# A hybrid decoder block in float32 on one core: 21 of 24 output pairs of the ma, mb and sb projections by seven block products

## The chip, the cores and the metric

The kernel runs on one core of one Trainium2 chip. The metric is device time in microseconds (us) of one execution, the median of several. Engines are named as the profile names them: PE is the tensor engine (PEld its weight loads), DVE the vector engine, ACT the scalar engine, POOL the general engine, SP the sync engine, which issues most DMAs.

## What is computed

A sequence of 512 tokens with 2048 channels, with 16 learned tokens in front (528 in all), goes through one layer. All is float32.

```
hn = rms_norm(h, norm_g)                       # h: 16 meta tokens, then x
z  = hn @ w_in                                 # 2048 x 14336
xa, sa, vb, gb, sb, ma, mb = split(z)          # seven times 2048 columns
ya = rg_lru(causal_conv4(xa)) * silu(sa)       # branch A, gates by 128 x 128 heads
pa = ya @ w_proj_a
yb = causal_conv31(vb * sigmoid(gb))           # branch B
yb = silu(layer_norm(yb)) * silu(sb)
pb = yb @ w_proj_b
h  = h + (sigmoid(ma) * pa + sigmoid(mb) * pb) @ w_out
out = rms_norm(h, final_g)[16:]
```

## The kernel before

Channels lie on the 128 partitions, in 16 tiles; tokens lie along the free dimension. A float32 product is made of three passes of type float32r: every operand is cut into a high and a low part, and hi x hi, lo x hi and hi x lo are summed in PSUM. The normalised input stays in SBUF as x_hi and x_lo, 16 tiles of 528 columns; ya, later yb, as y_hi and y_lo, 16 tiles of 512.

Weights stream in chunks of 512 KB (4 input tiles x 256 output columns). SP loads a chunk into one of RING = 2 slots of raw once the low part of the chunk two before is cut; ACT cuts w_hi from it (cut_hi, L537) once the matmuls of the chunk two before are done; DVE cuts w_lo (cut_lo, L784); PE runs multiply (L369): for 4 input tiles and 2 output tiles first the two passes with w_hi (16 matmuls), then, after a wait for w_lo, the pass with w_lo (8 matmuls). Two output tiles are a pair; four chunks make a pair. Counting semaphores (hi_ready, lo_ready, multiplied) hold chunk numbers, so each engine runs its own queue in code order.

The stages, in the order of the code:

- *Eight branch bodies* of 16 chunks: xa, sa, gb, vb for one pair each. xa, gb and vb are computed for all 528 tokens, as two halves of 264 columns (all_tokens), sa for 512 (x_tokens). Beside them DVE runs the two causal convolutions (conv_b_taps for the pair before, 31 taps, spread by the table TAPS), the recurrence (a scan), and the cut of ya (cut, L796 and L799). Before each of the chunks 8 to 11 PE runs a gate_round (L398), for which c_hi and c_lo must be cut from the short convolution. At the end gate_vb (L981) waits for the whole body's matmuls. The results of the long convolution are spilled to DRAM by POOL.
- *Four a_body:* for each pair the ma projection (x_tokens) and the product of ya with w_proj_a (y_tokens); the sigmoid of ma times pa is spilled. The first also finishes the long convolution of the last pair. The mean of the layer norm comes from a matmul with a constant matrix (L440), the variance later (L478), followed by Sqrt on ACT (L698) and a reciprocal on DVE (L1027) in the first b_body.
- *Four b_body:* sb and mb (x_tokens), the layer norm, the two silu and the cut of yb into y_hi and y_lo.
- *Two bodies of w_proj_b* (y_tokens) with merge, which cuts the merged sum into the x tiles.
- *The output product:* tokens become the stationary operand (x_hi, x_lo), w_out the moving one (L508); the last quarter of w_out is kept as y_hi, y_lo and used at the end (L522), followed by the residual and the last norm.

## Time and profile before

| | us |
|---|---|
| median of 3 runs | 1856.15 |
| lowest, highest | 1855.87, 1856.15 |
| span of the profiled execution | 1854.9 |
| PE busy | 1835.9 |
| PE weight loads busy | 1606.7 |
| DVE busy | 1085.7 |
| ACT busy | 556.3 |
| moved by DMA | 201.55 MB |

The profile is of one execution. Its busy times add durations, and a matmul's duration includes the time until its result has left the array, so successive matmuls overlap; the distance between their starts tells what one costs. The chain of waits is followed back from the last instruction. In the timeline a number of instructions of one form that follow each other is one row, and the idle time before it and what ended it stand in brackets.

### The profile page before, as it was taken

How to read it: one execution, taken by the hardware profiler on the slowest of the kernel's cores; microseconds unless marked ns; L12 is line 12 of the kernel's file. 1: busy time of each engine (PE TensorE's matmuls, PEld its weight loads, DVE VectorE, ACT ScalarE, POOL GpSimd, SP SyncE). 2: the span in 40 equal slices, each digit the busy share in tenths (PEclk: the TensorE clock that was granted, in tenths of full speed). 3: DMA queues.
4: the chain of work that ended last, by engine and by line, in shares of the span. 5: the costliest groups of instructions: out<-in, count | busy, mean ns of one | idle time of the engine just before them, and what ended most of it. 6: DMA issues, size and time to landing. Idle time of an engine off the chain costs nothing.

```text
span 1854.9 us, 26126 instructions
## 1 busy us (share of the span) xinstructions
PE 1835.9 (99%) x10220; PEld 1606.7 (87%) x10220; DVE 1085.7 (59%) x1446; ACT 556.3 (30%) x716; POOL 82.7 (4%) x82
## 2 busy tenths in 40 slices
PE   8999999999999999999999999999999999999998
PEld 7899999999999999988888888888888888888886
DVE  7978787879797979786224243434334433433441
ACT  6542333232423242422213223222222221212322
POOL 5500000000000000000000000000000000000000
PEclk9999999999999999999999999999999999999999
DMA  5233323233323323233633333233332333336422
GB/s 187 80 97 92 99 89 107 90 97 96 101 91 94 104 85 102 90 102 115 210 106 114 102 112 103 91 102 91 95 98 90 101 125 124 114 114 210 145 88 91
DMA packets 169445, 201.55 MB, mean 109 GB/s; under 512 B 6192, under 2 KB 153776, under 8 KB 168752
## 3 DMA queue, kind: packets, MB, share of 16 engines
q1 hardware_dynamic: 163360, 176.68, 30.0%
q0 software_dynamic: 6032, 24.12, 3.9%
q8 instruction: 38, 0.62, 0.1%
q14 instruction: 15, 0.12, 0.0%
HBM read 188.19 MB, written 12.58 MB: 108 GB/s over the span
## 4 chain that ended last, share of the span: by engine, by line
PE 95%; DVE 3%; ACT 1%; issue 0%; DMA 0%; SPq 0%; DVEq 0%; ACTq 0%
PE psum L369 84%; PE psum L508 7%; PE psum L522 2%; PE psum L398 1%; DVE x_lo L874 1%; DVE w_lo L784 1%; DVE region L1103 0%; DMA raw<-in_w_in 0%; DVE region L843 0%; ACT w_hi L537 0%; DVE total L882 0%; DVE region L839 0%; ACT wide L568 0%; DVE x_lo L1097 0%; ACT region L773 0%
## 5 line engine op out<-in xcount | busy, mean ns | idle before, releaser
L369 PE MATMUL psum<-x_hi,w_hi 128*128 128x264 f32 (+1 forms) x2560 | 717.1, 329 | 5.0 <-issue 2.8
L369 PE MATMUL psum<-x_lo,w_hi 128*128 128x264 f32 (+1 forms) x2560 | 715.8, 328 | 0.0
L784 DVE TENSOR_TENSOR w_lo<-raw,w_hi 128x1024 fp32r<-128x1024 f32 x288 | 357.0, 1241 | 559.2 <-ACT w_hi L537 557.1
L537 ACT ACTIVATE w_hi<-raw 128x1024 fp32r<-128x1024 f32 x288 | 305.3, 1060 | 1110.0 <-PE psum L369 1030.6
L369 PEld LDWEIGHTS psum<-x_hi,w_hi 128*128 128x128 f32 x2560 | 432.0, 189 | 50.5 <-issue 4.0
L369 PEld LDWEIGHTS psum<-x_lo,w_hi 128*128 128x128 f32 x2560 | 431.6, 188 | 43.9 <-issue 0.5
L369 PE MATMUL psum<-x_hi,w_lo 128*128 128x264 f32 (+1 forms) x2560 | 458.4, 327 | 2.8 <-DVE w_lo L784 2.8
L369 PEld LDWEIGHTS psum<-x_hi,w_lo 128*128 128x128 f32 x2560 | 386.4, 188 | 47.0 <-DVE w_lo L784 3.4
L818 DVE SCALAR_TENSOR_TENSOR region<-region,conv_cols 128x512 f32<-128x512 f32 x480 | 326.6, 745 | 0.0
L369 PE MATMUL psum<-y_hi,w_hi 128*128 128x512 f32 x512 | 199.8, 390 | 0.0
L369 PE MATMUL psum<-y_lo,w_hi 128*128 128x512 f32 x512 | 199.3, 389 | 0.0
L369 PE MATMUL psum<-y_hi,w_lo 128*128 128x512 f32 x512 | 126.4, 389 | 0.0
L369 PEld LDWEIGHTS psum<-y_hi,w_hi 128*128 128x128 f32 x512 | 96.1, 188 | 20.4 <-issue 0.2
L369 PEld LDWEIGHTS psum<-y_lo,w_hi 128*128 128x128 f32 x512 | 96.1, 188 | 20.3 <-issue 0.2
L369 PEld LDWEIGHTS psum<-y_hi,w_lo 128*128 128x128 f32 x512 | 96.1, 188 | 19.9
L508 PE MATMUL psum<-w_hi,x_hi 128*128 128x512 f32 x192 | 75.6, 394 | 0.0
L508 PE MATMUL psum<-w_hi,x_lo 128*128 128x512 f32 x192 | 75.3, 392 | 0.0
L1196 DVE TENSOR_TENSOR w_lo<-raw,w_hi 128x1024 fp32r<-128x1024 f32 x24 | 29.4, 1224 | 75.4 <-ACT w_hi L759 75.3
L759 ACT ACTIVATE w_hi<-raw 128x1024 fp32r<-128x1024 f32 x24 | 25.4, 1060 | 91.4 <-PE psum L508 51.6
L508 PE MATMUL psum<-w_lo,x_hi 128*128 128x512 f32 x192 | 48.3, 393 | 0.0
L508 PEld LDWEIGHTS psum<-w_hi,x_hi 128*128 128x128 f32 x192 | 36.1, 188 | 8.5
L508 PEld LDWEIGHTS psum<-w_lo,x_hi 128*128 128x128 f32 x192 | 36.1, 188 | 8.2
(150 smaller groups left out, 1000.7 us busy)
## 6 DMA issues: line engine op xcount, KB each, us to landing
raw<-in_w_in SPq DMA_DIRECT2D x224, 512.0 KB, 3.5
raw<-in_w_proj_a SPq DMA_DIRECT2D x32, 512.0 KB, 3.4
raw<-in_w_proj_b SPq DMA_DIRECT2D x32, 512.0 KB, 3.4
raw<-in_w_out SPq DMA_DIRECT2D x32, 512.0 KB, 3.8
region<-in_x_channels SPq DMA_DIRECT2D x8, 512.0 KB, 7.5
conv_b_spill<-region POOLq DMA_DIRECT2D x8, 512.0 KB, 3.2
gated_a_spill<-wide POOLq DMA_DIRECT2D x8, 512.0 KB, 3.5
region<-conv_b_spill POOLq DMA_DIRECT2D x4, 1024.0 KB, 10.8
```

The source lines that it names most:

```text
L369: last = pe.matmul(psum[:, bank, 0:width], weights[:, p % RING, k, m * P:(m + 1) * P], operand[part][:, 4 * group + k, t0:t0 + width], sta ...
L398: last = pe.matmul(psum[:, 6 + g, 0:HALF], weights[:, g, n // 2, :], part[:, :], start=weights is gate_hi and part is c_hi, stop=weights i ...
L508: last = pe.matmul(psum[:, banks + t, :], part[:, 2 * g + k, META + t * P:META + (t + 1) * P], weights[:, k, :], start=g == 0 and k == 0 a ...
L522: last = pe.matmul(psum[:, 4 * (LAST % 2) + t, :], part[:, j, META + t * P:META + (t + 1) * P], weights[:, j, :], start=j == 0 and part is ...
L537: act.activation(w_hi[:, p % RING, :], raw[:, p % RING, :], ACT.Copy).then_inc(hi_ready, 1)
L759: act.activation(to, raw[:, i % RING, :].rearrange("p (k n) -> p k n", k=2), ACT.Copy)\
L784: dve.tensor_tensor(w_lo[:, p % RING, :], raw[:, p % RING, :], w_hi[:, p % RING, :].bitcast(F32), ALU.subtract).then_inc(lo_ready, 1)
L818: ins = dve.scalar_tensor_tensor(conv_b[:, t, :], moved, w, conv_b[:, t, :], ALU.mult, ALU.add)
L874: dve.scalar_tensor_tensor(x_lo[:, j, META:T], channels[:, j, :], params[:, j, NORM_G:NORM_G + 1], x_hi[:, j, META:T].bitcast(F32), ALU.mu ...
L1196: dve.tensor_tensor(lo, raw[:, i % RING, :].rearrange("p (k n) -> p k n", k=2), hi.bitcast(F32), ALU.subtract).then_inc(lo_ready, 1)
```

## The change

Seven block products take the place of the eight of a 2 x 2 block multiplication. A pair's 2048 x 256 weights are cut into four blocks, by input half (8 tiles each) and output tile; the 512 tokens are cut into two halves of 256. The first STD = 3 pairs of the order ma, mb, sb are made as before; the other NV = 21 are units of seven products (A11, S2, S1, S3, A12, A22, S4), each over 8 input tiles with 256 columns. S1 to S4 are sums of weight blocks and are made on DVE for each unit. The token-side sums t_hi, t_lo (four blocks) are made once: t_sums, t_hi_of and t_lo_of in the branch bodies 1 to 7 and in the first plain chunks. They lie where y_hi and y_lo lie; so ya is spilled uncut by POOL and loaded and cut later (load_ya, ya_cut_hi, ya_cut_lo).

Three PSUM banks serve a unit. S2, S3 and A22 accumulate in one bank, A11 and A12 in another, S1 and S4 in the third, and between the products the intermediate values are read: copy_e1 and gate_c11 on ACT, read_u2, read_c22 (u3, then C22), read_c21 and read_c12 on DVE. PE waits for e1, u2, u3 and C22 in between. Weight blocks are loaded with 1 MB each into region, which the branch stage had used for its work tiles; the product operands have four slots, two of them in the unused quarter of the x tiles (cut_slots).

ma, mb and sb times yb are spilled. The layer norm reads the spilled convolution pair by pair into ln, once for the variance (centre_for_variance, square_ln, add_squares in units 1 to 9) and once for yb (centre, scale, silu_ln, gate_yb, from unit 14 on). Silu takes the place of a sigmoid and a product. Then follow 32 chunks of w_proj_a with ya, during which yb is loaded and cut into the x tiles, and 32 chunks of w_proj_b (x_tokens) with the merge, which now cuts into the y tiles. The output product takes y_hi, y_lo as the stationary operand and keeps its last quarter in the x tiles. The long convolution of the last pair runs beside 12 chunks with its own table of taps.

The core of the diff:

```diff
-        y_hi, y_lo = sb("y_hi", [P, CT, SEQ], F32R), sb("y_lo", [P, CT, SEQ], F32R)
+        t_hi, t_lo = sb("t_hi", [P, 4, KH, HS], F32R), sb("t_lo", [P, 4, KH, HS], F32R)
+        y_hi, y_lo = (t[:, :, :, :].rearrange("p b j n -> p (b j n)").rearrange("p (k s) -> p k s", k=CT)
+                      for t in (t_hi, t_lo))
...
+        def cut_slots(s):
+
+
+            if s < RING:
+                return [w[:, s, :].rearrange("p (r h n) -> p r h n", r=4, h=2) for w in (w_hi, w_lo)]
+            r = 4 * (s - RING)
+            return [x_part[:, r:r + 4, META + HS:].rearrange("p r (h n) -> p r h n", h=2) for x_part in (x_hi, x_lo)]
...
-        B_A, B_N, B_B, B_O = PAIRS, PAIRS + QUADS, PAIRS + 2 * QUADS, PAIRS + 2 * QUADS + CT // 8
-
+        STD, NV = 3, 3 * PAIRS - 3
+        C0 = PAIRS * BODY
+        W0 = C0 + 4 * STD
+        A0 = W0 + 7 * NV
...
+        def chunk_free(n):
+
+
+            if W0 <= n < W0 + 4:
+                return min(n, W0)
+            if A0 <= n < A0 + RING:
...
+            def load_blocks(v, h):
+
+
+                if v < 2:
+                    if v == 0:
+                        sp.wait_ge(ya_ready, CT)
+                    else:
+                        sp.wait_ge(vb_gated, CT)
+                        sp.wait_ge(conv_b_spilled, 16 * PAIRS)
+                        sp.wait_ge(summed, CT)
+                        sp.wait_ge(t_lo_ready, 2 * KH)
+                elif h == 0:
+                    sp.wait_ge(s4_ready, v - 1)
+                else:
+                    sp.wait_ge(lo_ready, W0 + 7 * (v - 1))
+                b = 2 * (v % 2) + h
+                sp.dma_start(blocks[:, b], w_in_v[:, KH * h:KH * (h + 1), ds(w_column(STD + v), 256)])\
+                    .then_inc(block_loaded[b], 16)
...
+            def product(v, q, bank, operand, more):
+
+
+                n = W0 + 7 * v + q
+                hi, lo = cut_slots(slot(n))
+
+                def passes(weights, parts, first, last):
+                    for k in range(KH):
+                        for part in parts:
+                            ins = pe.matmul(psum[:, bank, 0:HS], weights[:, k // 2, k % 2, :], operand(part, k),
+                                            start=first and k == 0 and part == 0, stop=last and k == KH - 1,
+                                            skip_group_check=more)
+                    return ins
+
+                pe.wait_ge(hi_ready, n + 1)
+                passes(hi, (0, 1), not more, False)
+                pe.wait_ge(lo_ready, n + 1)
+                passes(lo, (0,), False, True).then_inc(multiplied, 1)
...
+            def unit(v):
+
+
+                w = STD + v
+                a, b, c = (3 * (w % 2) + n for n in range(3))
+                if v < 2:
+                    pe.wait_ge(o_gated, v + 2)
+                    pe.wait_ge(vb_gated, CT)
+                else:
+                    pe.wait_ge(c11_ready, v - 1)
+                product(v, A11, a, x_block(0, 0), False)
+                wait(pe, c21_ready, v - 1)
+                if v == 0:
+                    pe.wait_ge(t_hi_ready, 2 * KH)
+                    pe.wait_ge(t_lo_ready, 2 * KH)
+                product(v, S2, b, t_block(T_T2), False)
+                wait(pe, c12_ready, v - 1)
+                product(v, S1, c, t_block(T_N1), False)
+                if v == 0:
+                    pe.wait_ge(summed, CT)
+                    pe.wait_ge(average_ready, 1)
+                    pe.matmul(psum[:, 7, :], average[:, :], total[:, :], start=True, stop=True).then_inc(mean_ready, 1)
+                pe.wait_ge(u2_ready, v + 1)
+                product(v, S3, b, t_block(T_T3), True)
+                if v == PAIRS + 1:
+                    pe.wait_ge(summed, 2 * CT)
+                    pe.matmul(psum[:, 6, :], average[:, :], total[:, :], start=True, stop=True).then_inc(var_ready, 1)
+                pe.wait_ge(e1_ready, v + 1)
+                product(v, A12, a, x_block(1, 0), True)
+                pe.wait_ge(u3_ready, v + 1)
+                product(v, A22, b, t_block(T_T4), True)
+                pe.wait_ge(c22_ready, v + 1)
+                product(v, S4, c, x_block(1, 1), True)
...
+            for w in range(STD):
+                if w == 1:
+                    pe.wait_ge(vb_gated, CT)
+                elif w == 2:
+                    pe.wait_ge(o_gated, 1)
+                for g in range(4):
+                    multiply(0, C0 + 4 * w + g, x_tokens((3 * (w % 2), 3 * (w % 2) + 1)), g)
+            for v in range(NV):
+                unit(v)
...
+            def operand_hi(v, q):
+
...
+                else:
+                    act.wait_ge({S1: s1_ready, S2: s2_ready, S3: s3_ready, S4: s4_ready}[q], v + 1)
+                act.wait_ge(multiplied, chunk_free(n))
...
+            def unit(v):
+                for q in range(7):
+                    if q == 1:
+                        if v:
+                            gate_c11(v - 1)
+                        else:
+                            gate_std(STD - 1)
+                    if q == 4:
+                        copy_e1(v)
+                        if v:
+                            gate_rest(v - 1)
+                    if q == 5 and STD + v > 2 * PAIRS:
+                        silu_ln(STD + v - 2 * PAIRS - 1)
+                    operand_hi(v, q)
+                    if q == 4 and v == PAIRS + 1:
                         act.wait_ge(var_ready, 1)
                         act.activation(psum[:, 6, :], psum[:, 6, :], ACT.Sqrt, bias=eps).then_inc(std_ready, 1)
-                    if p in (1, 9) and not (first and p == 1):
...
+            def t_sums(j):
+
...
+                r1 = steps(dve.tensor_tensor(sums_a, x_tile(x_hi, j), x_tile(x_lo, j), ALU.add))
+                r2 = steps(dve.tensor_tensor(sums_b, x_tile(x_hi, plus(j, KH)), x_tile(x_lo, plus(j, KH)), ALU.add))
+                steps.done(r1)
+                n1 = steps(dve.tensor_tensor(half(sums_a, 0), half(sums_a, 0), half(sums_a, 1), ALU.subtract))
+                steps.done(r2)
+                dve.tensor_tensor(half(sums_a, 1), half(sums_a, 1), half(sums_b, 1), ALU.subtract)\
+                    .then_inc(t_summed, 1)
+                steps.done(n1)
+                t2 = steps(dve.tensor_tensor(half(sums_b, 1), half(sums_b, 1), half(sums_a, 0), ALU.add))
+                steps.done(t2)
+                dve.tensor_tensor(half(sums_b, 0), half(sums_b, 0), half(sums_b, 1), ALU.subtract)\
+                    .then_inc(t_summed, 1)
...
+            def sum_s2(v):
+
+
+                a11, a21, a12, a22, s3 = winograd_operands(v)
+                dve.wait_ge(s1_ready, v + 1)
+                dve.tensor_tensor(a11, a11, a21, ALU.add).then_inc(s2_ready, 1)
...
+            def read_c22(v):
+
+                w = STD + v
+                dve.wait_ge(multiplied, W0 + 7 * v + S3 + 1)
+                dve.tensor_tensor(u3, bank(v, 1), e1, ALU.subtract).then_inc(u3_ready, 1)
+                dve.wait_ge(u3_ready, v + 1)
+                dve.wait_ge(o_spilled[w % 2], 16 * (w // 2))
+                dve.tensor_tensor(quarter(v, 1, 1), u3, bank(v, 2), ALU.subtract).then_inc(c22_ready, 1)
+
...
+            def unit(v):
+                i = STD + v - 2 * PAIRS - 1
+                if v:
+                    read_c22(v - 1)
+                operand_lo(v, A11)
+                sum_s2(v)
+                if 2 <= v <= PAIRS + 1:
+                    add_squares(v - 2)
+                operand_lo(v, S2)
+                if v:
+                    read_c21(v - 1)
+                if i >= 0:
+                    centre(i)
+                operand_lo(v, S1)
+                if v:
+                    read_c12(v - 1)
+                if i >= 0:
+                    scale(i)
+                operand_lo(v, S3)
+                if 1 <= v <= PAIRS:
+                    centre_for_variance(v - 1)
+                operand_lo(v, A12)
+                sum_s4(v)
+                read_u2(v)
+                operand_lo(v, A22)
+                if v == 0:
+                    dve.wait_ge(mean_ready, 1)
+                    dve.memset(total[:, :], 0.0).then_inc(total_cleared, 1)
+                    dve.wait_ge(total_cleared, 1)
+                if v == PAIRS + 1:
+                    dve.wait_ge(std_ready, 1)
+                    dve.reciprocal(psum[:, 6, :], psum[:, 6, :]).then_inc(rstd_ready, 1)
+                    dve.wait_ge(rstd_ready, 1)
+                if v + 1 < NV:
+                    sum_s3(v + 1)
+                if i >= 0:
+                    gate_yb(i)
+                operand_lo(v, S4)
+                if v + 1 < NV:
+                    sum_s1(v + 1)
```

## Rows read from the trace of the kernel before

**Rows 1.** The page: busy time by engine, and the span in 40 slices.
```profile
PE 1835.9 (99%) x10220; PEld 1606.7 (87%) x10220; DVE 1085.7 (59%) x1446; ACT 556.3 (30%) x716; POOL 82.7 (4%) x82
PEclk9999999999999999999999999999999999999999
GB/s 187 80 97 92 99 89 107 90 97 96 101 91 94 104 85 102 90 102 115 210 106 114 102 112 103 91 102 91 95 98 90 101 125 124 114 114 210 145 88 91
```

**Rows 2.** The chain that ended last: start us, us, what.
```profile
82.61 7.47 PE psum L369 x48
...
643.16 0.72 PE psum L398 x6
...
650.46 5.86 PE psum L369 x48
...
898.30 0.86 PE psum L440 x2
...
1141.42 527.83 PE psum L369 x2304
1669.25 133.03 PE psum L508 x576
1802.28 44.49 PE psum L522 x192
```

**Rows 3.** Timeline of PE and ACT: start us, us, instruction; chunk starts.
```profile
788.18 0.40 PE L369 MATMUL psum<-x_hi,w_hi 128*128 128x512 f32 x1
793.73 0.39 PE L369 MATMUL psum<-x_hi,w_hi 128*128 128x512 f32 x1
...
1003.21 0.39 PE L369 MATMUL psum<-y_hi,w_hi 128*128 128x512 f32 x1
1003.41 1.06 ACT L537 ACTIVATE w_hi<-raw 128x1024 fp32r<-128x1024 f32 x1 [3.89 <-PE psum L369]
1008.65 0.40 PE L369 MATMUL psum<-x_hi,w_hi 128*128 128x512 f32 x1
```

**Rows 4.** Timeline of DVE: start us, us, instruction, idle before.
```profile
639.91 0.43 DVE L858 TENSOR_TENSOR c_lo<-region,c_hi 128x264 fp32r<-128x264 f32 x1
640.25 2.73 DVE L818 SCALAR_TENSOR_TENSOR region<-region,conv_cols 128x512 f32<-128x512 f32 x4
...
788.38 1.32 DVE L981 TENSOR_TENSOR region<-region,psum 128x528 f32<-128x528 f32 x2 [4.04 <-PE psum L369]
...
797.00 4.06 DVE L818 SCALAR_TENSOR_TENSOR region<-region,conv_cols 128x512 f32<-128x512 f32 x6
800.97 1.22 DVE L784 TENSOR_TENSOR w_lo<-raw,w_hi 128x1024 fp32r<-128x1024 f32 x1
...
999.06 1.23 DVE L784 TENSOR_TENSOR w_lo<-raw,w_hi 128x1024 fp32r<-128x1024 f32 x1 [3.02 <-ACT w_hi L537]
1000.20 0.68 DVE L1005 TENSOR_TENSOR region<-region,psum 128x512 f32 x1
1000.80 0.68 DVE L1010 TENSOR_TENSOR total<-total,psum 128x512 f32<-128x512 f32 x1
```

**Rows 5.** Windows: one branch body, busy us by engine.
```profile
166.24:261.62 95.38, 95.38 (x698) 91.28 (x698) 80.22 (x113) 32.43 (x44) 2.17 (x3) 1.00 0.32 97
```

**Rows 6.** Groups by shape, the reciprocal: busy us, mean ns of one, idle before.
```profile
L1027 DVE RECIPROCAL psum<-psum 128x512 f32<-128x512 f32 x1 | 3.4, 3358 | 0.0
```

**Rows 7.** Timeline of ACT around the square root of the variance.
```profile
1136.29 1.28 ACT L698 ACT_TABLE_LOAD   x1
1141.45 0.66 ACT L698 ACTIVATE psum<-psum,stats 128x512 f32<-128x512 f32 x1 [3.89 <-PE psum L478]
```

**Rows 8.** Windows: the granted clock (third number from the end) in body 0.
```profile
82.80:86.30 3.50, 3.50 (x19) 3.50 (x20) 3.28 (x4) 2.08 (x4) 2.50 (x2) 0.59 0.43 142
```

**Rows 9.** The page's DMA issues: count, KB each, us to landing.
```profile
region<-conv_b_spill POOLq DMA_DIRECT2D x4, 1024.0 KB, 10.8
wide<-gated_a_spill POOLq DMA_DIRECT2D x8, 512.0 KB, 4.1
```

More of the change, by code:

```diff
@@ new lines, in ya_tokens @@
+            def ya_tokens(banks):
+                return [[(bank, SEQ, (y_hi, y_lo), 0, y_tile)] for bank in banks]
+            def product(v, q, bank, operand, more):
[12 more added lines that the diff above has]
+                passes(lo, (0,), False, True).then_inc(multiplied, 1)
@@ new lines, in operand_hi @@
+            def operand_hi(v, q):
+                n = W0 + 7 * v + q
+                a11, a21, a12, a22, s3 = winograd_operands(v)
+                one, two = 2 * (v % 2), 2 * (v % 2) + 1
+                if q == A11:
+                    act.wait_ge(block_loaded[one], 16 * (v // 2 + 1))
+                elif q in (A12, A22):
+                    act.wait_ge(block_loaded[two], 16 * (v // 2 + 1))
+                else:
+                    act.wait_ge({S1: s1_ready, S2: s2_ready, S3: s3_ready, S4: s4_ready}[q], v + 1)
+                act.wait_ge(multiplied, chunk_free(n))
+                source = {A11: a11, S2: a11, S1: a21, S3: s3, A12: a12, A22: a22, S4: a12}[q]
+                act.activation(cut_slots(slot(n))[0], source.rearrange("p (r h) n -> p r h n", h=2), ACT.Copy)\
+                    .then_inc(hi_ready, 1)
@@ L708, in b_body @@
[L708 to L716 removed]
+                    if q == 5 and 1 <= v <= PAIRS:
+                        square_ln(v - 1)
@@ L943, in branch_end @@
                     if p == 13:
+                        if taps is not None:
+                            t_lo_of(i + -1)
                         dve.wait_ge(gates_read, plus(4 * i, 4))
@@ L966, in branch_end @@
                             dve.wait_ge(sa_silu, plus(2 * i, t + 1))
-                            gate.append(steps(dve.tensor_tensor(
-                                silu_sa[:, t, :], rec[:, t, META:T], silu_sa[:, t, :], ALU.mult)))
-                        cut([silu_sa[:, t, :] for t in range(2)], gate, y_hi, y_lo, 2 * i, slice(0, SEQ), lru_out)
+                            dve.tensor_tensor(silu_sa[:, t, :], rec[:, t, META:T], silu_sa[:, t, :], ALU.mult)\
+                                .then_inc(ya_ready, 1)
                     if taps is not None:
@@ new lines, in operand_lo, with sum_s3 @@
+            def operand_lo(v, q):
+                n = W0 + 7 * v + q
+                a11, a21, a12, a22, s3 = winograd_operands(v)
+                source = {A11: a11, S2: a11, S1: a21, S3: s3, A12: a12, A22: a22, S4: a12}[q]
+                hi, lo = cut_slots(slot(n))
+                dve.wait_ge(hi_ready, n + 1)
+                dve.tensor_tensor(lo, source.rearrange("p (r h) n -> p r h n", h=2), hi.bitcast(F32), ALU.subtract)\
+                    .then_inc(lo_ready, 1)
+            def sum_s3(v):
+                a11, a21, a12, a22, s3 = winograd_operands(v)
+                dve.wait_ge(block_loaded[2 * (v % 2)], 16 * (v // 2 + 1))
+                dve.tensor_tensor(s3, a11, a21, ALU.add).then_inc(s3_ready, 1)
@@ L1184, in _ @@
-            steps.at(start + (QUADS - 1) * PER_B_BODY)
-            for q in range(CT // 8):
-                for p in range(BODY):
-                    cut_lo(B_B + q, p)
-                    if p % 4 == 1 and (q, p) != (0, 1):
-                        n = 4 * q + p // 4 - 1
-                        merge(n // 4, n % 4)
+            TAPS[:] = [2, 3, 3, 3, 3, 3, 3, 3, 3, 3, 2, 0]
+            assert sum(TAPS) == KB
+            taps = [None, None]
+            for n in range(C0, W0):
+                p = n - C0
+                chunk_lo(n)
+                if p == 0:
+                    one_step(dve.tensor_copy(conv_cols[:, :, :], lru_cols[:, :, :]))
+                    t_sums(KH - 1)
+                conv_b_taps(PAIRS, p, taps)
+                if p == 4:
+                    t_lo_of(KH - 1)
+                if p == 11:
+                    sum_s3(0)
+                    sum_s1(0)
+                    add_total(PAIRS)
@@ new lines, in _ @@
+            for v in range(NV):
+                unit(v)
+            read_c22(NV - 1)
+            for u in range(4):
+                ya_cut_lo(u)
+            for m in range(4 * PAIRS):
+                chunk_lo(A0 + m)
+                if m == 0:
+                    read_c21(NV - 1)
+                    for u in range(4, 8):
+                        ya_cut_lo(u)
+                if m == 1:
+                    read_c12(NV - 1)
+                if m == 2:
+                    centre(PAIRS - 1)
+                    scale(PAIRS - 1)
+                if m == 4:
+                    gate_yb(PAIRS - 1)
+                if m % 4 == 1 and m > 4:
+                    gate_pa(m // 4 - 1)
+                if m >= 7 and (m - 7) % 3 == 0 and (m - 7) // 3 < PAIRS:
+                    yb_cut_lo((m - 7) // 3)
```

696 lines of the change are left out of this document (410 added, 286 removed).

## The prediction

> **What bounds the kernel now.** I read the busy shares and the granted clock first: the tensor engine is busy 1835.9 of 1854.9 us at full clock in nearly every slice, the vector engine 1085.7, the scalar engine 556.3 [rows 1]. The chain of waits then says the same by time: after the first branch body it is matmuls almost alone, at last 527.83 us in one piece for three fifths of the touched stretch and 133.03 + 44.49 us for the output [rows 2]. So a stage costs what its matmuls cost, until something makes the tensor engine wait. The change touches 881.1 us of it (788.2 [rows 3] to 1669.3 [rows 2]): 160 chunks of 24 matmuls.
>
> The price of a matmul is the distance of starts in the timeline, not its duration (the 390 ns are latency). A chunk of 24 x 512 columns takes 1008.65 - 1003.21 = 5.44 us with the y tiles as moving operand and 793.73 - 788.18 = 5.54 us with the x tiles: 227 and 231 ns [rows 3]. A chunk of 48 x 264 columns takes 5.86 us [rows 2] = 122.1 ns each. 264 columns at 2.4 GHz are 110.0 ns, so 12.1 ns come on top. In the gate rounds the stationary operand changes after one or two matmuls, and 6 still take 0.72 us, 120 ns each [rows 2].
>
> The other two engines: 1024 columns cost 1.06 us on the scalar engine [rows 3] and 1.23 us on the vector engine; back to back the vector engine's next instruction starts 1.14 us later, after 512 columns 0.60 us, after 264 columns 0.34 us, and six taps take 3.98 us [rows 4]. From the start of the next chunk's matmuls to the scalar engine's answer a hand-over takes 0.20 us (1003.21 to 1003.41) [rows 3].
>
> **The change, part by part.** *Matmuls.* One of the 24 pairs costs 4 x 5.54 = 22.1 us. Seven products of 24 matmuls x 256 columns replace it in 21 pairs. No row shows 256 columns. From below: half of a 512-column one, 114.5 ns; from above: 122.1 ns, if 264 columns already are at some floor. I take 122.1 - 8 / 2.4 = 118.8 ns, the nearest row less its 8 columns: a product 2.85 us, a unit 19.95 us, saving 21 x 2.2 = 46 us. Exactly: the 96 x-chunks (531.4 us) become 12 chunks (66.4) and 21 units (419.0): **-46.0 us**, bounds -61 and -34.
>
> The Trainium skill (TensorE: Matmul & The Clock Gate, Back-to-back issue gap) gives columns / 2.4 GHz + 2.5 ns when warm. By it 256 columns would take 109 ns and a unit 18.3 us, an estimate. The rows at 264 and 512 columns stand 10 to 15 ns above that rule, so here the measurement decides.
>
> *Which tiles are where.* yb now lies in the x tiles, so the last 32 projection chunks cost 5.54 instead of 5.44 us: **+3.0 us**. In the output stage the stationary operand moves to the y tiles: 133.03 / 576 = 231 ns [rows 2] should become 227, **-2.4 us** (bounds 0 and -2.4); the last 192 matmuls keep one x operand.
>
> *Branch stage.* Per body the vector engine gets the token sums after chunk 0 (2 x 0.60 + 4 x 0.34 + 0.3 us of waits between them: 2.85 us) and two 512-column subtractions (1.2 us), and loses the casts and subtractions of ya (2.0 us); the scalar engine gets 1.2 us. The vector engine is 80.2 of 95.4 us busy there [rows 5]. What is late next is c_lo for the first gate round: written by 640.34, needed at 643.16 [rows 4, 2]. If all 2.85 us arrived there, it would be ready at 643.19, just in time; part of it vanishes in the 15.2 us that the engine idles per body: **0 us**. Without that cover it would be up to 3 us in each of 7 bodies.
>
> *The 12 plain chunks.* All 31 taps of the last pair, t_sums and t_lo now lie in 12 chunks instead of 16. The worst point is the first: gate_vb starts at 788.38 [rows 4], then chunk 0, a copy, t_sums (to 793.7), two taps (to 796.0), chunk 1 cut by 797.2. The tensor engine wants it at 793.73 + 3.70 = 797.4. After that each step is 1.14 + 3.98 = 5.12 us against 5.54, and the lag falls. **0 us**, margin 0.2.
>
> *Into the units.* chunk_free makes the first product's hi cut wait for all plain chunks: 0.2 + 1.06 us. Then sum_s2 waits for the lo cut and the hi cut of S2 for sum_s2: 0.7 us more. **+2 us**.
>
> *Inside a unit* I walk the queues in code order, with 0 = end of A11 on the tensor engine; S2, S1, S3, A12, A22, S4 end at 2.85, 5.7, 8.55, 11.4, 14.25, 17.1. Vector work per unit: 7 cuts and 4 sums x 1.14, five bank reads x 0.36 = 14.4 us; +2.5 us for variance (v 2 to 8), +3.5 us for normalising and gating (v from 14). The fullest case, v from 14: read_u2 starts 4.6 (needed by 5.7), cut A22 4.96, sum_s3 6.1, gate_yb 7.24, cut S4 8.38, sum_s1 9.52, u3 10.66 to 11.1 (the tensor engine wants it at 11.4), sum_s2 12.64 to 13.9, then the vector engine idles 1.1 us for the scalar engine's S2 cut, S2 15.0, S1 17.65, S3 20.3, A12 at 22.28 instead of 21.44. So the vector loop takes 19.1 us against 19.95: **0 us**, but the u3 hand-over has only 0.3 us. Each microsecond missed there is 7 us.
>
> *The variance.* Before, Sqrt and the 3.36 us reciprocal [rows 6] ran beside matmuls that did not need them. Now in unit 9 the reciprocal stands in the vector queue ahead of sum_s3, cut S4, sum_s1 and the u3 of the same unit, and A22 waits for u3. Mean matmul 8.55 to 9.4 (0.86 us [rows 2]), Sqrt to 10.1 (the table load comes before its wait [rows 7]), hi cut of A22 to 11.2, its lo cut, reciprocal 12.35 to 15.75, sum_s3, cut S4, sum_s1, u3 done at 19.6; A12 ended at 12.25. Stall **7.3 us**. Idle time this long costs clock too: after partly idle microseconds the granted clock was 0.59 from 82.8 to 86.3 us and a 5.86 us chunk took 7.47 [rows 8, 2]: **+1.6 us**.
>
> *Into the ya stage.* After S4 of the last unit ends at 17.1 us, ya's first lo tiles (14), chunk 0 (hi 12.6, lo 15.2) and chunk 1 (hi 18, lo 21.3, wanted at 26) are there. The four 1 MB ya loads go out at 4.6 and 8.4 us at the latest; four such loads took 10.8 us together, one of 512 KB some 4 [rows 9]. **0 us**, bound +4.
>
> *DMA.* A unit loads 2 MB, spills 0.5 and loads up to 0.5: 3 MB in 20 us, 157 GB/s; 46 us slices reached 210 [rows 1]. The blocks are requested 16 us before sum_s3 wants them. **0 us**.
>
> Sum against the profiled span: 1854.9 - 46.0 + 3.0 - 2.4 + 2.0 + 7.3 + 1.6 = 1820.4 us. The median lies 1.25 us above the span: **1822 us**.
>
> **Rivals.**
> 1. *Cheaper matmuls, the vector engine bounds.* At 114.5 ns a unit would be 19.24 us; but the units from v = 14 stop at the 19.1 us loop. For it: 512 columns cost no more than 231. Against: the 264-column rows. 21 x 0.7 us less: about 1807 us. By the issue gap of the Trainium skill's page (TensorE: Matmul & The Clock Gate) the vector loop would be the bound too.
> 2. *Hand-overs are missed, or 256 columns cost what 264 do.* 122.1 ns makes 20.5 us a unit, +12 us; u3 late by 1 us in 7 units, +7 us; one late buffer at each stage border, +4 us. For it: margins of 0.2 and 0.3 us in a walk whose steps are good to 0.1 us each. Between 1830 and 1848 us.
> 3. *Slower: the vector loop takes the place of the matmuls in all units.* u2, u3 and C22 stand between products, so a slow vector engine stops the tensor engine at once. The unit must lose 34 / 21 = 1.6 us, so reach 21.6 us; it needs the strided 256-column and PSUM-broadcast forms, which no row shows, at 1.4 instead of 1.14 us (14 of them, 3.6 us on the 19.1 us loop: 22.7 us, some 1880 us with the walk's waits). Against: the cut from contiguous rows takes 1.23 us and an operation that reads PSUM (L1005) no more than one that does not [rows 4], and units v < 14 have 1 to 3.5 us to spare.
> 4. *It does not do what it says:* NV = 21 units of seven products, and each product has 24 matmuls; the code says so. No chance given.
>
> Only a matmul dearer than 128.5 ns (118.8 + 34.2 / 3.528, with 3528 matmuls) would turn the sum. The gate rounds, at 120 ns with loads that change, speak against that.
>
> **How the numbers follow.** Forecast 0.52 (1814 to 1830), rival 1 0.10, rival 2 0.27, rival 3 0.07, close to no change (several costs of rival 2 at once) 0.04. Range 1808 to 1846: it leaves out rival 3 and the edges of 1 and 2. A measurement of this kernel tells 0.2% (3.7 us) from no change: faster 0.89, same 0.04, slower 0.07.
>
> **What would show it.** Product starts 2.85 us apart and units 19.95 us; no wait in the branch bodies (95.4 us each); 1 to 2 us before the first product; one wait of about 7 us before A22 of unit 9 with the reciprocal as its cause and a clock below 1 behind it; nearly none elsewhere. It is wrong if the tensor engine waits for u3, u2 or C22 in every unit, if 256 columns start 122 ns apart or more, or if the branch bodies grow.

## The result and the profile after

The kernel after takes **1823.19 us** (median of 4 runs, 1821.83 to 1824.23), the kernel before 1856.15 us in the same series: ratio 0.9822, 95% interval 0.9808 to 0.9836. It is 33.0 us (1.8%) faster; 1822 was predicted. Its profiled execution spans 1822.7 us; it was the slowest of the four (1824.23 us), so the trace below is of an execution 1.0 us above the median.

The page of after (busy us with its share of the span, the data moved in 40 slices of the span, one DMA group with its count, KB each and median us to landing):

```profile
PE 1791.8 (98%) x11732; PEld 1646.7 (90%) x11732; DVE 1279.1 (70%) x1610; ACT 666.3 (37%) x838; POOL 120.8 (7%) x134
GB/s 186 74 110 94 110 95 107 104 98 104 109 92 109 93 107 101 89 145 162 153 161 150 149 96 152 155 156 144 208 168 153 136 116 116 124 108 219 144 88 93
aux<-conv_b_spill POOLq DMA_DIRECT2D x24, 512.0 KB, 4.5
```

Beside [rows 1]: 1512 more matmuls, but 44 us less of tensor time; the vector engine has 193 us more work, the scalar engine 110 us more, and the slices of the units move some 150 GB/s instead of some 100. The tensor engine is busy 98% instead of 99%: a little of the gain has turned into waits.

The chain that ended last, from the end of the branch stage on (start us, us, what):

```profile
855.89 1.07 ACT w_hi L909
856.98 1.23 DVE w_lo L1324
858.21 1.15 DVE region L1344
859.38 1.07 ACT w_hi L909
860.58 5.94 PE psum L566 x48
866.52 0.86 PE psum L603 x2
867.38 182.13 PE psum L566 x1536
1049.52 0.87 PE psum L608 x2
1051.00 1.06 ACT w_hi L909
1053.22 3.37 DVE psum L1450
1057.76 1.22 DVE w_lo L1324
1058.98 1.14 DVE region L1337
1060.50 61.53 PE psum L566 x504
...
1240.61 8.72 DMA aux<-conv_b_spill
...
1262.98 25.86 PE psum L566 x216
1288.84 350.97 PE psum L532 x1536
1639.81 130.60 PE psum L719 x576
1770.41 44.52 PE psum L733 x192
```

L566 is the matmul of the seven products, L532 that of plain chunks, L719 and L733 are the output. Three places are new against [rows 2]. Operand cuts stand in the chain where the units begin (855.89 to 860.58). In the middle a chain of scalar and vector work with the reciprocal (L1450) in it takes the place of matmuls. Near the end of the units a DMA appears, the load of the spilled conv_b into aux. Between 1122.04 and 1262.98 us the chain runs from unit to unit over the general engine's spills and loads, and the tensor engine's own timeline shows matmuls there, with small delays in units 16, 17 and 19. Elsewhere matmuls stand back to back: 182.13 / 1536 = **118.6 ns** for each of 256 columns.

All long waits of the tensor engine in this stretch, from its timeline, and the vector engine's longest on that DMA; the brackets say how long the engine sat idle and for whom:

```profile
857.09 0.36 PE L566 MATMUL psum<-x_hi,w_hi 128*128 128x256 f32 x1 [1.30 <-ACT w_hi L909]
...
860.58 0.36 PE L566 MATMUL psum<-t_hi,w_hi 128*128 128x256 f32 x1 [0.43 <-ACT w_hi L909]
...
1060.50 0.58 PE L566 MATMUL psum<-t_hi,w_hi 128*128 128x256 f32 x1 [7.29 <-DVE aux L1369]
...
1249.36 1.22 DVE L1400 TENSOR_TENSOR aux<-aux,psum 128x1024 f32<-128x1024 f32 x1 [1.75 <-DMA aux<-conv_b_spill]
```

The length of each unit, from the start of its first matmul to that of the next unit's first, worked out from the timeline:

```
kernel   unit 0   units 1-8, 10-15, 18, 20   unit 9   unit 16   unit 17   unit 19   all 21
after     21.50   19.87 to 19.99              29.97    20.61     20.37     20.52     431.6 us
```

Unit 0 also holds the mean's matmul (0.86 us) and the wait of 0.43; unit 9 the variance's matmul (0.87). The kernel before has these two matmuls too, in other places.

### The profile page after: what moved, and what is told of

Same layout as the page of the kernel before. It is cut to its first block, busy times and chain, and to the rows that moved or that the text cites. A ratio compares the mean times of both kernels' runs of the same rounds, so it can differ in the third digit from the quotient of the medians.

```text
span 1822.7 us, 28896 instructions
## 1 busy us (share of the span) xinstructions
PE 1791.8 (98%) x11732; PEld 1646.7 (90%) x11732; DVE 1279.1 (70%) x1610; ACT 666.3 (37%) x838; POOL 120.8 (7%) x134
## 4 chain that ended last, share of the span: by engine, by line
PE 87%; issue 7%; DVE 4%; ACT 1%; DMA 1%; POOL 0%; SPq 0%; POOLq 0%; ACTq 0%; DVEq 0%
PE psum L532 60%; PE psum L566 15%; PE psum L719 7%; PE psum L733 2%; PE psum L623 1%; DVE x_lo L1197 1%; DVE w_lo L1090 1%; DVE region L1516 1%; DMA aux<-conv_b_spill 0%; DMA region<-in_x_channels 0%; DVE region L1166 0%; ACT w_hi L748 0%; DVE w_lo L1324 0%; POOL aux L440 0%; POOL conv_b_spill L436 0%
## 5 line engine op out<-in xcount | busy, mean ns | idle before, releaser
L532 PE MATMUL psum<-x_hi,w_hi 128*128 128x264 f32 (+1 forms) x2144 | 553.0, 316 | 8.5 <-ACT w_hi L748 3.8
L532 PE MATMUL psum<-x_lo,w_hi 128*128 128x264 f32 (+1 forms) x2144 | 552.0, 316 | 0.0
L532 PEld LDWEIGHTS psum<-x_hi,w_hi 128*128 128x128 f32 x2144 | 353.7, 189 | 36.1 <-issue 7.3
L532 PEld LDWEIGHTS psum<-x_lo,w_hi 128*128 128x128 f32 x2144 | 353.5, 188 | 25.9 <-issue 0.2
L532 PE MATMUL psum<-x_hi,w_lo 128*128 128x264 f32 (+1 forms) x2144 | 354.8, 315 | 2.0 <-DVE w_lo L1090 2.0
L532 PEld LDWEIGHTS psum<-x_hi,w_lo 128*128 128x128 f32 x2144 | 308.3, 188 | 28.3 <-DVE w_lo L1090 2.4
L748 ACT ACTIVATE w_hi<-raw 128x1024 fp32r<-128x1024 f32 x128 | 135.7, 1060 | 435.7 <-PE psum L532 399.4
L1315 DVE TENSOR_TENSOR w_lo<-raw,w_hi 128x1024 fp32r<-128x1024 f32 x76 | 93.1, 1224 | 211.4 <-ACT w_hi L893 211.4
L1090 DVE TENSOR_TENSOR w_lo<-raw,w_hi 128x1024 fp32r<-128x1024 f32 x128 | 161.1, 1259 | 58.8 <-ACT w_hi L748 58.6
L893 ACT ACTIVATE w_hi<-raw 128x1024 fp32r<-128x1024 f32 x76 | 80.6, 1061 | 301.3 <-PE psum L532 273.2
L532 PE MATMUL psum<-t_lo,w_hi 128*128 128x512 f32 x256 | 99.6, 389 | 0.0
L532 PE MATMUL psum<-t_hi,w_hi 128*128 128x512 f32 x256 | 99.6, 389 | 0.0
L566 PE MATMUL psum<-t_hi,w_hi 128*128 128x256 f32 x336 | 84.3, 288 | 8.0 <-DVE aux L1369 7.3
L566 PE MATMUL psum<-t_lo,w_hi 128*128 128x256 f32 x336 | 83.8, 286 | 0.0
L1633 DVE TENSOR_TENSOR w_lo<-raw,w_hi 128x1024 fp32r<-128x1024 f32 x24 | 29.4, 1226 | 74.7 <-ACT w_hi L1063 74.7
L566 PE MATMUL psum<-t_hi,x_hi 128*128 128x256 f32 x336 | 81.6, 282 | 0.1
L566 PE MATMUL psum<-t_lo,x_hi 128*128 128x256 f32 x336 | 80.9, 280 | 0.0
```

The source lines that it names most:

```text
L532: last = pe.matmul(psum[:, bank, 0:width], weights[:, s, k, m * P:(m + 1) * P], operand[part][:, place(4 * group + k), t0:t0 + width], sta ...
L566: ins = pe.matmul(psum[:, bank, 0:HS], weights[:, k // 2, k % 2, :], operand(part, k), start=first and k == 0 and part == 0, stop=last and ...
L748: act.activation(w_hi[:, p % RING, :], raw[:, p % RING, :], ACT.Copy).then_inc(hi_ready, 1)
L893: act.activation(w_hi[:, slot(n), :], raw[:, slot(n), :], ACT.Copy).then_inc(hi_ready, 1)
L1090: dve.tensor_tensor(w_lo[:, p % RING, :], raw[:, p % RING, :], w_hi[:, p % RING, :].bitcast(F32), ALU.subtract).then_inc(lo_ready, 1)
L1315: dve.tensor_tensor(w_lo[:, slot(n), :], raw[:, slot(n), :], w_hi[:, slot(n), :].bitcast(F32), ALU.subtract).then_inc(lo_ready, 1)
```

## Experiments

In all of them the kernel before, run on the same chip, took 1855.8 to 1856.2 us. Line numbers of an experiment's rows are those of its own file. The diffs are against the kernel after.

**1. Is it the reciprocal that stops unit 9?** It moves two units later, behind a point where nothing waits for it.

```
 def unit(v) on the vector engine
+                if v == PAIRS + 3:          # after read_c12(v - 1)
+                    dve.wait_ge(std_ready, 1)
+                    dve.reciprocal(psum[:, 6, :], psum[:, 6, :]).then_inc(rstd_ready, 1)
+                    dve.wait_ge(rstd_ready, 1)
...
-                if v == PAIRS + 1:
-                    dve.wait_ge(std_ready, 1)
-                    dve.reciprocal(psum[:, 6, :], psum[:, 6, :]).then_inc(rstd_ready, 1)
-                    dve.wait_ge(rstd_ready, 1)
```

> The reciprocal of the standard deviation leaves the vector queue of unit 9 and stands in unit 11, behind the read of C12; the square root stays in unit 9. Theory (two delays in a row: the scalar engine waits for the variance matmul before it cuts A22, then the reciprocal): the wait before A22 falls from 7.4 us by the reciprocal's 3.4 to about 4.0 us; unit 9 takes 26.5 us instead of 30.0, or 24.8 if so short a wait leaves the clock up; the whole 1818 to 1820 us. Rival A (the reciprocal alone is the cause): no wait is left, unit 9 takes 20.8 us. Rival B (the time comes back in unit 11): unit 11 grows by up to 3 us; by my walk it does not, since units 10 to 13 have 3 us of spare vector time.

Measured: 1819.37 us (1817.82 to 1820.99), 3.8 us below after, ratio to before 0.980 (0.9784 to 0.9817). Unit 9 takes 27.37 us, 2.6 less than in after; 26.5 was expected, or 24.8 with the clock up. Unit 11, where the reciprocal now stands, keeps its 19.87 us. The rest of the 3.8 us does not come from the edit: in the profiled execution the first unit alone starts 1.1 us earlier than in after. Timeline of its tensor engine in unit 9:

```profile
1055.99 0.58 PE L566 MATMUL psum<-t_hi,w_hi 128*128 128x256 f32 x1 [3.89 <-DVE aux L1369]
1056.37 0.41 PE L566 MATMUL psum<-t_lo,w_hi 128*128 128x256 f32 x1
1056.59 0.41 PE L566 MATMUL psum<-t_hi,w_hi 128*128 128x256 f32 x1
```

The wait falls from 7.29 to 3.89 us, by the 3.4 us of the reciprocal [rows 6]: the rest belongs to the square root, for which the scalar engine waited while the cut of A22 stood behind it. The rows also show what a wait of 3.9 us costs afterwards: starts 213 ns apart (1056.37, 1056.59, and so on to the end of the product) for 256 columns, which is the 1.2 GHz level, and the product took 5.29 us instead of 2.85, 2.4 us lost. Behind the wait of 7.29 it was 4.54 us in after (1.7 us lost), 4.39 in experiment 3 (1.5 us lost) and 4.95 to 5.29 us in experiments 4, 8 and 9 (2.1 to 2.4 us lost), which all have that wait. So the shorter wait, seen in one execution, left no smaller clock loss, and the loss behind one and the same wait varies by 0.9 us between executions.

**2. The square root as well.**

```
-                    if q == 4 and v == PAIRS + 1:
+                    if q == 4 and v == PAIRS + 2:
                         act.wait_ge(var_ready, 1)
                         act.activation(psum[:, 6, :], psum[:, 6, :], ACT.Sqrt, bias=eps).then_inc(std_ready, 1)
```
with the reciprocal as in experiment 1.

> As the run before, and the scalar engine's wait for the variance and its square root stand in unit 10. Theory: the whole wait goes, unit 9 takes 20.8 us (seven products and the variance matmul), no clock loss, 9.2 us less than the changed kernel: 1814 us. Rival: the vector queue of unit 9 is late for another reason, and 1 to 4 us of wait stay before A22.

Measured: 1813.56 us (1812.78 to 1815.21), ratio 0.9773 (0.9757 to 0.979). Unit 9 takes 20.84 us, of which 0.87 are the variance's matmul, and the chain runs through it:

```profile
1047.85 0.86 PE psum L608 x2
1048.71 62.53 PE psum L566 x528
```

The granted clock around the wait of after, by windows (window; its length; busy us of PE, PEld, DVE, ACT, POOL, with their instructions; granted clock; DMA share; GB/s):

```profile
1056.00:1058.00 2.00, 0.00 (x0) 0.00 (x0) 1.97 (x3) 0.00 (x0) 0.00 (x0) 0.82 0.00 0
1058.00:1060.50 2.50, 0.00 (x0) 0.00 (x0) 2.47 (x4) 0.00 (x0) 0.00 (x0) 0.50 0.14 39
1060.50:1064.00 3.50, 3.50 (x16) 3.50 (x17) 2.68 (x3) 0.79 (x1) 0.00 (x0) 0.50 0.81 277
1064.00:1068.00 4.00, 4.00 (x35) 4.00 (x34) 2.79 (x3) 1.33 (x2) 0.00 (x0) 0.99 0.00 0
```

A window of this experiment in the same unit, to be read in the same way:

```profile
1054.00:1058.00 4.00, 4.00 (x36) 4.00 (x35) 2.23 (x4) 1.71 (x2) 0.00 (x0) 1.00 0.00 0
```

The kernel after idles from 1053.2 us on. Its clock falls to half within the first of these windows, while the engine is idle (the 0.82 is an average over both levels), is at half for the first 3.5 us of matmuls and back behind them; without the wait it stays at full speed. The stall and its clock are worth 29.97 - 20.84 = 9.1 us, against 7.3 + 1.6 = 8.9 predicted. Both causes together are shown, since removing them removes all of it. Units 16, 17 and 19 are still 0.3 to 0.4 us longer than their neighbours here: that is another cause, experiment 4.

**3. The start of the units.** The first product's weights may go into their slot when the second last plain chunk is done, not the last.

```
             if W0 <= n < W0 + 4:
-                return min(n, W0)
+                return W0 - 1 if n == W0 else W0
```

> The hi cut of the first product waits for all plain chunks but the last, since its slot was last read by the chunk before the last. Theory: the 1.3 us before the first product and the 0.4 us before the second go, unit 0 starts 2.84 us products at once; 1.7 us less between the last plain chunk and unit 1. Rival: the hi cut of S2 waits for sum_s2 and for the sigmoid ahead of it in the scalar queue, and takes 0.5 to 1 us back before the second product.

Measured: 1820.39 us in one run. The last plain matmuls and the first of the products now stand without a gap:

```profile
853.27 1.99 PE L532 MATMUL psum<-x_hi,w_lo 128*128 128x512 f32 x8
855.10 0.28 PE L566 MATMUL psum<-x_hi,w_hi 128*128 128x256 f32 x1
```

Unit 0 takes 20.78 instead of 21.50 us: the wait of 0.43 for S2 goes too, with the slow first matmuls behind each wait. With the 1.30 us in front that is 2.0 us, the term that was put at +2.0.

**4. Why are units 16, 17 and 19 long?** The load of conv_b for the layer norm was queued on POOL behind a spill (L436), and the normalising vector operation L1400 waited for it. The two change places.

```
-                spill_o(w - 1)
                 if w - 1 >= 2 * PAIRS - 1:
                     i = w - 2 * PAIRS
                     pool.wait_ge(yb_ready, i)
                     pool.wait_ge(summed, 2 * CT)
                     load_ln(i)
+                spill_o(w - 1)
```

> From unit 13 on the general engine issues the load of the layer norm's next pair ahead of the spill of the pair before instead of behind it. Theory (units 16, 17 and 19 are longer by 0.7, 0.5 and 0.6 us because this load lands up to 1.7 us after the vector engine wants it): the load lands at least 1 us earlier, no wait before centring, and all units from 14 on take 19.9 us; 1.8 us less. Rival (the vector queue alone is too full for the u3 hand-over): the long units stay, wherever the load lands.

POOL's issues in after, in its timeline:

```profile
1239.89 0.73 POOL L436 DMA_DIRECT2D conv_b_spill<-wide  x1 [18.30 <-DVE wide L1411]
1240.61 0.73 POOL L440 DMA_DIRECT2D aux<-conv_b_spill  x1
```

The same in this experiment:

```profile
1239.58 0.73 POOL L440 DMA_DIRECT2D aux<-conv_b_spill  x1 [18.54 <-DVE wide L1411]
1240.30 0.73 POOL L436 DMA_DIRECT2D conv_b_spill<-wide  x1
```

Measured: units 16, 17 and 19 take 19.87 to 19.99 us like the others, and the vector engine no longer waits for this load. In after it waited six times, 7.2 us in all: the waits of 1.73, 1.36 and 1.75 us made units 16, 17 and 19 longer by 0.72, 0.38 and 0.65 us, those of 1.01 us and less cost nothing, so some 1.0 us of such a wait is covered. The single time, 1823.27 us, is no shorter than the median of after, but its span of 1821.7 us is 1.0 us shorter than the one in which these units were read (1822.7): of the 1.8 us won, 0.7 was lost in its unit 9 (30.64 us, a longer half-clock stretch) and 0.2 before the units. That the edit pays is shown by the units, here and in experiment 5, not by this time. The size varies: the same three units together are 1.8 us too long in after and 0.8 to 1.4 us in experiments 1, 2, 3, 8 and 9, and not at all in the two executions with the load first.

In after seven such loads, from 1159.82 us on, landed 7.6 to 9.0 us from their issue (the one above 8.72), against a median of 4.5 us for all 24; with the load first the seven took 4.4 to 6.9 us. The 0.73 us of the issue slot are thus the small part; the transfers that run beside the load are the large one. In after the spill is one of them, issued 0.73 us ahead, and a weight block of 1 MB the other, issued 0.14 us behind (1159.96 and 1240.75 us). One load with a spill ahead of it, but no block right behind (1132.76), landed in 4.94 us. So the spill alone does not make it late; how the delay divides between the two was not tested.

**5. All three edits together.**

> The three edits together: reciprocal and square root later, the first slot's wait one chunk shorter, the layer norm's load ahead of the spill. Theory (each removes its own wait and they do not share time): 9.2 + 1.7 + 1.8 = 12.7 us less than the changed kernel, 1810.5 us, ratio to the kernel before 0.975. Rival (the waits overlap or move to the next stage border): over 1814 us.

Measured: **1809.93 us** (1808.8 to 1810.49, 5 rounds), ratio to before 0.9751 (0.9738 to 0.9765). It is 13.3 us below after and the fastest version of this study. Its chain from the units on:

```profile
1045.51 0.86 PE psum L608 x2
1046.37 227.56 PE psum L566 x1920
```

No wait is left in 21 units; they take 419.96 us against 431.6 + 1.3 in after. So the vector engine isn't the bound in any unit. Its busy share of 71% on the page averages over all stages and does not tell this; experiment 6 shows how little is free in the units from 14 on.

**6. How full is the vector loop of a unit?** One more vector operation of 1024 columns (1.14 us) in each unit up to v = 18, writing values that the next sum overwrites.

```
                 if v + 1 < NV:
                     sum_s1(v + 1)
+                if v < NV - 2:
+                    dve.tensor_tensor(spare, fixed, fixed, ALU.add).then_inc(spare_done, 1)
```

> One more vector operation of 1024 columns (1.14 us, a result that nothing reads) behind sum_s1 in the units 0 to 18. Theory of the walk (slack per unit: over 1.4 us before u3 for v up to 13, 0.3 us from v = 14): units 10 to 13 and 2 to 8 stay at 19.9 us; units 14 to 18 wait 0.9 us for u3 each and take 20.8 us; unit 9 waits 1.1 us more. Rival A (the vector engine is 88% busy in this stage, so one operation fits everywhere): all units stay at 19.9. Rival B (the vector engine is the hidden bound): all units grow by 1.1 us.

Measured: units 1 to 8 and 10 to 13 stay at 19.9 us, units 14 to 18 take 20.78 to 20.86. From its chain:

```profile
1225.80 0.35 DVE aux L1370
1226.19 8.83 PE psum L567 x72
```

Each unit from 14 to 18 now waits once for u3 (L1370) and is longer by 0.87 to 0.96 us than one without a wait: the walk of the prediction gave u3 a margin of 0.3 us for v from 14, and 1.14 - 0.3 = 0.84. Neither rival holds, neither that all units stay nor that all grow. All 21 units take 435.7 instead of 431.6 us (five times 0.9, 0.8 more in unit 9, 0.5 in unit 0, less the 1.8 us by which units 16, 17 and 19 were late in after), the total is 1828.14 us. So the queue walk was right to 0.1 us, and a vector loop 6% longer would have cost in the full units alone.

**7. What sets the price of a 256-column matmul?** The eight lo-weight matmuls of each product take 128 columns instead of 256, and half of that term of the result is missing.

```
+                        cols = P if weights is lo else HS
-                            ins = pe.matmul(psum[:, bank, 0:HS], weights[...], operand(part, k),
+                            ins = pe.matmul(psum[:, bank, 0:cols], weights[...], operand(part, k)[:, 0:cols],
```

> Leaves work out: the lo pass of each of the seven products takes 128 instead of 256 token columns, so half of the smallest term is missing. Theory (a matmul costs its columns at 2.4 GHz plus 12 ns): the 128-column matmuls start 65 ns apart, a product takes 2.43 us, units 10 to 13 take 17.0 us; from unit 14 the vector loop of 19.1 us becomes the bound. Rival (the load of new weights sets a floor near the 256-column time): the starts stay over 100 ns apart and every unit takes over 19 us.

Measured: 1817.40 us; units 1 to 8 and 10 to 14 take 19.49 to 19.54 us. So the theory fell and the rival held. Units 15 to 19 take 19.7 to 20.5 us, with waits that were not followed up. Timeline of a product's end, matmuls (PE) and weight loads (PEld), and of the same matmuls at the 1.2 GHz level, behind the wait of unit 9:

```profile
1094.11 1.01 PE L567 MATMUL psum<-t_hi,w_lo 128*128 128x128 f32 x8
1094.95 0.33 PE L567 MATMUL psum<-x_hi,w_hi 128*128 128x256 f32 x1
...
1096.77 0.97 PEld L567 LDWEIGHTS psum<-x_hi,w_lo 128*128 128x128 f32 x8
...
1059.96 0.31 PE L567 MATMUL psum<-t_hi,w_lo 128*128 128x128 f32 x1
1060.06 1.47 PE L567 MATMUL psum<-t_hi,w_lo 128*128 128x128 f32 x6
```

Halving the columns saved 19.92 - 19.5 = 0.4 us per unit over 56 matmuls, 7 ns each, where "columns at 2.4 GHz and 12 ns more" asks for 53 ns. The loads (one lasts 0.19 us) start (0.97 - 0.19) / 7 = 111 ns apart. So that rule of the prediction fell below 256 columns: about 111 ns is a floor here. Two more readings say that the weight loads set it, of which each matmul has one. The second narrow matmul of a product starts only 60 ns behind the first (the mean of 35 products), when its weights are in place already, and only the ones behind it 112 ns apart, as the loads do. And at the 1.2 GHz level the same: 0.10 us from the first to the second (1059.96, 1060.06), then 213 ns each, as far apart as matmuls of 256 columns at that level, though the columns alone ask for half. At 256 columns and full clock the stream stands only 7 ns above the floor. The Trainium skill (TensorE: Matmul & The Clock Gate, LDWEIGHTS (loading the stationary operand)) gives columns of the stationary operand / 1.2 GHz, 107 ns for 128 columns; these rows agree within 4 ns at full clock, but at the 1.2 GHz level the loads start 213 ns apart.

**8 and 9. What covers the token sums in the branch stage?** The first two additions of t_sums (0.60 us each) are repeated once (+1.2 us of vector work per body), then three times (+3.6 us), with the same results.

```
+                for n in range(2):          # 9: range(4)
                     r1 = steps(dve.tensor_tensor(sums_a, ..., ALU.add))
                     r2 = steps(dve.tensor_tensor(sums_b, ..., ALU.add))
```

> The first two additions of the token-side sums (512 columns each, about 0.60 us each) are done twice in every branch body and in the first plain chunk; results are unchanged. That is 1.2 us more of vector work ahead of the operand pass that the gate matmuls wait for. Cover theory: in the branch bodies that pass ends 2.4 us before it is wanted, so the bodies stay at 95.4 us and only the stage of the 12 plain chunks, where the margin is 0.3 to 1.3 us, grows, by about 0 to 1 us. Total 1823 to 1824.5. Rival (the vector work was on the path all along, and the zero of the prediction came out by chance): each of the bodies grows by 1.2 us, some 8 us in all, about 1831.

> The same two additions are done four times: 3.6 us more of vector work per body. Cover theory: 2.4 us of it are covered, the bodies grow by 3.6 - 2.4 = 1.2 us each (some 8 us over seven) and the plain chunks by 2.3 to 3.3 us, total 1833 to 1836. Rival of full price: 3.6 us per body, about 1850. Rival of no price (the tensor engine catches up elsewhere in the body): 1823.

Measured: 1823.48 and 1837.39 us. Chain of experiment 8 over one body, where the first row and the last are 95.40 us apart as in after:

```profile
165.86 0.74 PE psum L623 x6
...
261.26 0.74 PE psum L623 x6
```

The same two rows of experiment 9:

```profile
167.27 0.96 PE psum L623 x6
...
264.19 0.95 PE psum L623 x6
```

And the one wait of its tensor engine between them, from the timeline:

```profile
228.10 2.23 PE L532 MATMUL psum<-x_hi,w_lo 128*128 128x264 f32 x16 [1.03 <-DVE w_lo L1090]
```

1.2 us vanish, and of 3.6 us 1.03 come out as idle time. The body grows by 96.92 - 95.40 = 1.52 us. Start by start against a body of after, about 1.3 us of it lie at this wait (the first matmul behind it is slow as well) and 0.25 us before the gates: their first weight load starts 0.07 us behind the end of c_lo (360.99 and 361.06 in the next body), so that operand is late too. The cover is thus 2.3 us (3.6 - 1.3). Seven bodies give 10.6 us. In the plain chunks, where the prediction saw the smallest margin, the first cut that matters came 0.80 us late in experiment 8 (timeline of the tensor engine):

```profile
798.10 2.11 PE L532 MATMUL psum<-x_hi,w_lo 128*128 128x512 f32 x8 [0.80 <-DVE w_lo L1322]
```

and 3.20 us late in experiment 9:

```profile
811.23 2.12 PE L532 MATMUL psum<-x_hi,w_lo 128*128 128x512 f32 x8 [3.20 <-DVE w_lo L1322]
```

1.2 - 0.80 and 3.6 - 3.20 both leave a cover of 0.4 us there, against 0.2 predicted. The single time of experiment 8 is only 0.3 us above the median of after, that of experiment 9 14.2 us, 1.4 us above the 1833 to 1836 us expected for it. The zero of the branch stage was thus a real cover and no cancelling.

## Why the prediction was right

Its terms against the trace of after; the sum was made for the span, 1820.4 us, and the span is 1822.7.

```
step                              predicted     measured        difference
first body and bodies 1 to 7      788.18        789.29          +1.1
12 plain chunks                    66.4          66.5           +0.1
into the units (both waits)         2.0           1.3 + 0.4     -0.3
price of a 256-column matmul      118.8 ns      118.6 ns        -0.7 over 3528
start of unit 0, after its waits     0            0.3           +0.3
stall in unit 9                     7.3           7.3             0
its clock                           1.6           1.8           +0.2
hand-overs from v = 14               0            1.8           +1.8
proj a and b, 64 chunks           351.4         351.0           -0.4
output                             -2.4          -2.4             0
```

The span moved from 1854.9 to 1822.7 us; the median lies 1.2 us above the forecast. Of the prediction's readings, the chunk of 5.54 us is 5.55 by its two rows and the six taps of 3.98 us are 3.97, and c_lo at 643.19 us would have been 0.03 us late and not just in time; none of these moves a term.

**The matmul price** carried the forecast: 46 us of gain hang on it, with bounds from -61 to -34. The nearest row less its 8 columns gave 118.8 ns [rows 2], and 118.6 was measured. The choice was good, but the picture behind it (a constant on top of the columns) is only half true. From 256 to 512 columns it holds roughly (12 ns on top at 256 and 264, 14 to 18 at 512), and below 256 it does not, as experiment 7 shows. The rival at 114.5 ns (half of a 512-column matmul) fell because the part that doesn't shrink with the columns is paid in full; the one at 122.1 ns because 8 columns fewer did save their 3.5 ns. The issue gap of the Trainium skill (TensorE: Matmul & The Clock Gate, Back-to-back issue gap), 109 ns by estimate, which the page gives for an isolated matmul, is not reached in this stream.

**The variance** was found by walking the queues, not from any row of before: the reciprocal had been free for as long as no matmul waited for what lay behind it. Place (A22 of unit 9), cause and size came out, and experiments 1 and 2 split the stall into 3.4 us for the reciprocal and 3.9 for the square root's chain. The walk's end, 7.3 us, could come out so closely because each of its steps has nearly the same duration each time (7.29 to 7.30 us idle in the five traces with the same vector queue). The 1.6 us for the clock was taken from a stretch in body 0 and is partly luck: the same wait lost 1.5 to 2.4 us in these traces.

**The branch stage** cost nothing, as said: its bodies are 95.4 us [rows 5], and the gates' operand is there with 2.4 us to spare:

```profile
641.39 0.43 DVE L1181 TENSOR_TENSOR c_lo<-region,c_hi 128x264 fp32r<-128x264 f32 x1
...
644.25 0.74 PE psum L623 x6
```

(The first row is of the vector engine's timeline, the second of the chain.) The prediction named this operand as the one that is late next. Experiment 9 bears that out in part: with 3.6 us more the cut of a weight block in the middle of the body comes late by more (1.3 us), and c_lo, relieved by that wait, by 0.25 us.

**The step that was mis-sized** is the DMA: "requested 16 us before they are wanted, 0 us". That looked at the weight blocks on SP's queue. The load for the layer norm goes out on POOL behind a spill of 512 KB of the same unit and just ahead of a weight block, took up to 9.0 us to land, and the vector engine waited for it; three units lost 0.4 to 0.7 us each, 1.8 us in all. Rival 2 had foreseen missed hand-overs of u3 for v from 14, but as the vector engine's own doing, at 7 us; here a DMA caused them, in 3 of 7 units, at u3 and at u2, and 1.0 us of each wait was covered. Experiment 4 shows the cause.

**Part of the difference is the run.** The start of the kernel, whose code is not touched, moved by 1.1 us, and among the kernels here with the same branch stage the last plain chunk ended between 854.0 and 856.0 us. Where that start differs was not looked into. Rival 3 (a vector loop of 21.6 us or more) fell on its condition: the strided and PSUM forms took 1.22 us alone and 1.14 back to back, as the plain ones do. Experiment 6 gives its true distance: 0.3 us in the full units.

## What to carry to other kernels

Where small matmuls replace larger ones, price them by the distance of starts of the nearest width that the trace shows, and ask at which width the weight load takes over: Strassen's seven products paid here because 256 columns cost little more than half of what 512 do; one level further down, the matmuls would be 1.75 times as many at 111 instead of 118.6 ns (an estimate from these rows, not tried). Then walk the queues of the other engines for everything that was free only because nobody waited behind it; here one square root and one reciprocal cost 9.1 us of a 46 us gain, and moving them by one and two units gave it back. Put a load that is wanted soon ahead of a spill that nobody waits for, and ask what other transfer starts beside it.

## What was not expected of the hardware

A matmul of 128 columns with a weight load of its own starts about 111 ns after the one before, hardly cheaper than the 118.6 ns of 256 columns, and at the 1.2 GHz level both start 213 ns apart. And a wait of 3.9 us already halved the clock behind it: 2.4 us were lost after it in the one execution that shows it, 1.5 to 2.4 us after 7.3 us of waiting in five, so that the loss in clock did not shrink with the wait. The granted clock had fallen to 0.50 while the engine was still idle.
